# Running both gate/up products of a pair of expert items ahead of its transposes and down products

## The chip, the cores and the metric

The kernel runs on one core of one Trainium2 chip. The metric is the device time of one execution in microseconds (us), given as the median of the runs shown. The durations below come from one profiled execution of the same kernel.

## What is computed

One inference step of a two-layer decoder on 256 prompt tokens and 8 x 4 sample tokens, T = 288 tokens of width D = 1024 in all. Layer 0 mixes tokens with a chunked spatial-gating MLP, layer 1 with block-sparse attention over a paged cache. Each mixer is followed by a mixture of experts, which is the part this change touches:

```python
# x: the 288 normalised tokens; 16 experts, two per token, all inside one group of four
a   = einsum('nd,edf->nef', x, w_gate)      # w_gate, w_up: 16 x 1024 x 256
b   = einsum('nd,edf->nef', x, w_up)
hid = silu(a) * b * gates[:, :, None]       # gates: zero but for the two chosen experts
y   = einsum('nef,efd->nd', hid, w_down)    # w_down: 16 x 256 x 1024
h   = h + y
```

Everything is float32. One expert's weights are 1 MB (gate), 1 MB (up) and 1 MB (down).

## The kernel before

**Items and pairs.** The tokens of an expert are served in *items* of up to 64 slots. Each of the 16 experts has one item; experts with more than 64 tokens get further items, planned at run time. Items are worked in pairs `i`, with `u` = 0 and 1 and the running number `q = 2i + u`. In the profiled execution layer 0 has 16 items (8 pairs) and layer 1 has 18 (9 pairs); each L1090 group of 32 matmuls is one item. A float32 matmul of the source counts as two instructions.

**One item on TensorE** (`pair`, L1080 to L1109). It waits for the item's gate and up weights, for the transposed token rows `x_slotsT[:, u]` (`xt_sb`) and for the `hid` tile of two items before. Then come the gate/up products (L1090, 32 instructions into bank 2+u). After the first item of a pair stands `table_of(i + 3)` (L1061, 12 small matmuls that make the index table of a later pair). Then `rows_up` (L1070) transposes the gathered token rows of the *next* item. Then two transposes of `hid` (L1101, into bank 4) and, after DVE has copied them to `hidT`, the down products (L1108, 8 instructions into bank 5+u). `dn` is raised at their end. TensorE works in program order.

**One item on ACT** (`experts`, L576 to L583). It waits for `gu`, makes `silu` (L580), waits for `dn` of the *same* item, then for the scatter that last used the buffer, and copies the result to `y_slots` (L583). Then comes the next item. `ready_for(ACT.Silu)` (L549) loads the table once in a pair.

**One item on DVE** (L846 to L854). `hid` = `silu` x up x gate (L848) once `silued` is raised, `x_tile` (L828: the next item's transposed rows out of PSUM), the copy to `hidT` (L852), and the copy of the output indices (L854). At the end of a pair stands the index arithmetic of pair `i+3` (L798 to L807), at its beginning a one-hot of 6 instructions (L780).

**One pair on POOL** (L477 to L494). For u = 0 and 1: wait until the earlier gather has landed, copy the indices (L462), wait until `rows_up` has emptied the buffer (`xt`), and issue the gather of the *next pair's* rows (L466, 128 half rows of 2 KB, an indirect DMA). Then for u = 0 and 1: wait for the copy of L583 and issue the scatter (L492). The loop then starts again, so the next pair's gathers stand behind this pair's second scatter.

**Weights.** SP issues the loads. There are four sets of weight buffers: `ew_in`/`ew_down` (two) and the halves `pre_in`/`pre_down` (two). The first four items' weights are loaded before the expert stage. Items 4 and 5 go to `ew`, 6 and 7 to the halves, and all from item 8 on to the two `ew` buffers alone. A gate/up load is issued when the products that last read its buffer are done (`hold(gu)`), a down load likewise (`hold(dn)`). The order is in(u=0), down(0), in(1), down(1). So the loads of items 4 to 7 are released by items 0 to 3, those of 8 and 9 by items 4 and 5, and those of 10 by item 8.

**Before and behind.** Ahead of the loop TensorE makes two tables and the transposes of item 0's rows (`rows_up(0, 16, 0)`). After the last pair SP waits for the last scatters and loads the rows of `y` back.

## Time and profile before

| | |
|---|---|
| median of 3 runs | 822.12 us (822.06 to 829.37) |
| span of the profiled execution | 826.3 us |
| TensorE (PE) busy | 642.1 us, 78% |
| DVE busy | 291.2 us, 35% |
| ACT busy | 160.0 us, 19% |
| POOL busy | 138.6 us, 17% |
| moved by DMA | 187.77 MB, mean 227 GB/s |
| on the chain that ended last | PE 61%, DMA 15%, DVE 10% |

The span of the profiled execution lies between the fastest and the slowest of the runs, 4.2 us above their median. Busy shares are means over stages with different limits, so the table says little of the expert stages by itself; they run from about 185 to 317 us (layer 0) and from 648 to 798 us (layer 1). Matmul ends are modelled, and a matmul group can overlap the one before it by some 0.1 us.

### The profile page before, as it was taken

The page shows a single profiled execution, that of the slowest core. Times are in us where ns is not written, and L with a number is a line of the kernel's source. Part 1 is how long each engine was busy: PE and PEld are TensorE (multiplying, and loading weights), DVE is VectorE, ACT ScalarE, POOL GpSimd, SP SyncE. Part 2 cuts the span into 40 slices and gives each one's busy share as a digit, 9 for nine tenths or more (in the row PEclk, how much of TensorE's full clock was granted, in tenths as well). Part 3 has the DMA queues.
Part 4 walks back from the last instruction along what each step waited for, and adds up shares of the span by engine and source line. Part 5 has one row for each costly group of instructions (what it writes and reads, how often), then busy time and mean ns, then how long its engine had stood idle before and what let it go on. Part 6 is the DMA issues. An engine that isn't in the chain of part 4 may idle for free.

```text
span 826.3 us, 12476 instructions
## 1 busy us (share of the span) xinstructions
PE 642.1 (78%) x4123; PEld 435.9 (53%) x4123; DVE 291.2 (35%) x916; ACT 160.0 (19%) x336; POOL 138.6 (17%) x224
## 2 busy tenths in 40 slices
PE   5899999839888763799988857766987788876740
PEld 3677667525555442576667526445765455534420
DVE  2202211473334221537747341332126443333214
ACT  2123101111212111111125321211113121222100
POOL 0000000022323220131114001420000223222212
PEclk9999959968999997599999986976998799999995
DMA  9964400426999994970019563973923399999933
GB/s 349 288 229 175 137 23 1 153 72 235 369 369 314 371 360 147 402 304 0 1 52 367 179 212 128 337 268 152 349 81 132 118 370 374 324 374 366 361 127 123
DMA packets 114729, 187.77 MB, mean 227 GB/s; under 512 B 11996, under 2 KB 82190, under 8 KB 114694
## 3 DMA queue, kind: packets, MB, share of 16 engines
q1 hardware_dynamic: 103174, 158.71, 55.4%
q0 software_dynamic: 11520, 28.60, 9.5%
q8 instruction: 20, 0.33, 0.2%
q14 instruction: 15, 0.12, 0.0%
HBM read 182.95 MB, written 13.76 MB: 238 GB/s over the span
## 4 chain that ended last, share of the span: by engine, by line
PE 61%; DMA 15%; DVE 10%; issue 5%; SPq 5%; ACT 3%; DVEq 0%; POOLq 0%; ACTq 0%
PE PS L1005 24%; PE PS L1090 12%; DMA ew_in<-in_moe_w_up 10%; PE PS L1108 5%; PE PS L996 3%; PE PS L1301 2%; DMA half_a<-in_cache_k 2%; DMA zT<-y_rows 2%; SPq L292 2%; SPq L305 2%; PE PS L1176 1%; PE PS L1265 1%; PE PS L1021 1%; SPq L294 1%; PE PS L1061 1%
## 5 line engine op out<-in xcount | busy, mean ns | idle before, releaser
L1090 PE MATMUL PS<-ew_in,zT 128*64 128x256 f32 x832 | 99.8, 394 | 21.9 <-DMA ew_in<-in_moe_w_up 18.7
L1005 PE MATMUL PS<-hT,half_a 128*128 128x288 f32 x384 | 98.1, 414 | 4.0 <-DVE hT L678 3.1
L1090 PEld LDWEIGHTS PS<-ew_in,zT 128*64 128x64 f32 x832 | 67.4, 142 | 62.4 <-issue 43.7
L1005 PEld LDWEIGHTS PS<-hT,half_a 128*128 128x128 f32 x384 | 73.2, 193 | 27.8 <-issue 3.7
L848 DVE SCALAR_TENSOR_TENSOR zT<-PS,slot_gates,zT 64x256 f32<-64x256 f32 x34 | 16.5, 485 | 163.6 <-ACT zT L580 159.1
L1005 PE MATMUL PS<-hT,half_b 128*128 128x288 f32 x256 | 66.9, 421 | 3.3 <-DVE hT L678 3.3
L1108 PE MATMUL PS<-ew_down,zT 128*64 128x512 f32 x208 | 50.4, 601 | 17.3 <-issue 17.3
L492 POOL DMA_INDIRECT y_rows<-zT,out_idx x34 | 34.3, 1010 | 155.7 <-ACT zT L583 155.7
L1005 PEld LDWEIGHTS PS<-hT,half_b 128*128 128x128 f32 x256 | 50.1, 197 | 19.5 <-issue 3.7
L1265 PE MATMUL PS<-cst,half_a 128*128 128x128 f32 x256 | 40.3, 308 | 17.7 <-DMA half_a<-in_cache_k 10.2
L1265 PEld LDWEIGHTS PS<-cst,half_a 128*128 128x128 f32 x256 | 32.1, 157 | 33.3 <-issue 15.5
L466 POOL DMA_INDIRECT zT<-h_rows,in_idx x38 | 39.7, 1045 | 58.5 <-PE PS L1070 27.0
L583 ACT COPY zT<-PS 128x512 f32<-128x512 f32 x34 | 19.9, 585 | 125.5 <-PE PS L1108 125.5
L472 POOL DMA_DIRECT2D h_rows<-tokbuf x2 | 1.7, 830 | 244.7 <-ACT tokbuf L571 244.7
L549 ACT ACT_TABLE_LOAD x24 | 30.8, 1283 | 25.6 <-DVE pairs L820 24.4
L555 ACT ACTIVATE sq<-xT 128x288 f32<-128x288 f32 x32 | 13.6, 442 | 112.9 <-DVE xT L685 86.0
L1005 PE MATMUL PS<-zT,half_a 128*128 128x288 f32 x128 | 34.1, 426 | 0.0
L1108 PEld LDWEIGHTS PS<-ew_down,zT 128*64 128x64 f32 x208 | 14.9, 136 | 33.5 <-issue 33.5
L580 ACT ACTIVATE zT<-PS 64x256 f32<-64x256 f32 x34 | 12.8, 377 | 100.2 <-PE PS L1090 100.2
L675 DVE RECIPROCAL rec<-std 128x288 f32<-128x288 f32 x5 | 9.8, 1953 | 57.6 <-ACT std L559 57.6
L1005 PEld LDWEIGHTS PS<-zT,half_a 128*128 128x128 f32 x128 | 25.6, 201 | 7.4
L685 DVE TENSOR_TENSOR xT<-PS,xT 128x288 f32<-128x288 f32 x16 | 7.3, 457 | 61.8 <-PE PS L1005 61.8
(234 smaller groups left out, 892.5 us busy)
## 6 DMA issues: line engine op xcount, KB each, us to landing
ew_in<-in_moe_w_gate SPq DMA_DIRECT2D x26, 1024.0 KB
ew_in<-in_moe_w_up SPq DMA_DIRECT2D x26, 1024.0 KB
ew_down<-in_moe_w_down SPq DMA_DIRECT2D x26, 1024.0 KB, 12.4
half_a<-in_cache_k SPq DMA_DIRECT2D x64, 256.0 KB, 4.0
ew_in<-in_cache_v POOLq DMA_DIRECT2D x32, 256.0 KB, 6.8
half_b<-in_cache_v POOLq DMA_DIRECT2D x32, 256.0 KB, 5.6
half_a<-in_a_w_in SPq DMA_DIRECT2D x1, 4096.0 KB, 15.2
half_b<-in_a_w_in SPq DMA_DIRECT2D x1, 4096.0 KB, 25.3
```

The lines of the kernel that those rows point to most:

```text
L292: at = [eng.value_load(pages[0:1, bass.ds(b * NPAGE + j, 1)], min_val=0, max_val=NPOOL - 1) for j in pp]
L305: sp.dma_start(dst, src).then_inc(s, 16)
L466: pool.indirect_dma_start(out=x_slots[:, u, :], out_offset=None, in_=h_dram.rearrange("t (h n) -> (t h) n", h=2), in_offset=bass.IndirectO ...
L492: pool.indirect_dma_start(out=y_dram[l].rearrange("t k (h n) -> (t k h) n", h=2), out_offset=bass.IndirectOffsetOnAxis(ap=out_idx[u][:, 0: ...
L549: act.activation(spare[:, :], eps[:, :], func)
L583: act.copy(y_slots[:, u, :], PS[:, 5 + u, :]).then_inc(E[l]["y_sb"], 1)
L996: mm = pe.matmul(PS[:, 7, 0:T], mean_d[:, :], sq[:, k, :], start=(k == 0), stop=(k == KT - 1))
L1005: mm = pe.matmul(PS[:, bank, 0:T], w[:, k, col:col + P], src[:, k, :], start=(k == 0), stop=(k == KT - 1))
L1090: mm = pe.matmul(PS[f * SLOT:(f + 1) * SLOT, 2 + u, 0:EF], x_slotsT[:, u, k % 4, k // 4, :], w_in[u][:, k, f, :], start=(k == 0), stop=(k ...
L1108: mm = pe.matmul(PS[half * SLOT:(half + 1) * SLOT, 5 + u, :], hidT[:, f, :], w_down[u][:, f, half * HALF:(half + 1) * HALF], start=(f == 0 ...
L1265: mm = pe.transpose(PS[:, n % 2, a * P:(a + 1) * P], k_pages[:, bb % 2, n % NPAGE, a * P:(a + 1) * P], ident)
L1301: mm = pe.matmul(PS[a * HR:(a + 1) * HR, 5, bb * P:(bb + 1) * P], PdT[:, j, a * HR:(a + 1) * HR], v_pages[bb][:, j, a * P:(a + 1) * P], st ...
```

## The change

In each pair TensorE now does: gate/up of item 0, gate/up of item 1, the table, then for each item the `hid` transposes, `rows_up`, and the down products. `rows_up` now serves the item two further on, `q + 2`, with the same `u`, and waits for that item's gather, `in{u}` at `16 * (i + 2)`; so `rows_up(1, 16, 1)` and `x_tile(1, 2)` are added ahead of the loop. On DVE `x_tile` comes behind the copy to `hidT` instead of ahead of it. ACT gets one more wait, since both `silu` share a buffer; its order is otherwise as it was. POOL's code is unchanged. SP's loads come in the order in(0), in(1), down(0), down(1). The last wait before the `y` rows are loaded counts one tile more.

```diff
--- before.py
+++ after.py
@@ -349,33 +349,33 @@
 
 
                 with sp.Fori(1, QUADS) as i:
-                    for u in range(4):
-
-                        w_in, w_down = (ew_in, ew_down) if u < 2 else (pre_in, pre_down)
-                        hold(E[l]["gu"], 4 * i - 3 + u)
-                        expert_in(l, 4 * i + u, w_in[u % 2], E[l][f"w{u}"] if u < 2 else s_pre[u % 2])
-                        hold(E[l]["dn"], 4 * i - 3 + u)
-                        expert_down(l, 4 * i + u, w_down[u % 2], E[l][f"wd{u}"] if u < 2 else s_pre[u % 2])
-
-                def item(e, u, before):
-
-                    hold(E[l]["gu"], before + 1)
-                    expert_in(l, e, ew_in[u], E[l][f"w{u}"])
-                    hold(E[l]["dn"], before + 1)
-                    expert_down(l, e, ew_down[u], E[l][f"wd{u}"])
-
-                for u in range(2):
-                    item(4 * QUADS + u, u, 4 * QUADS - 4 + u)
+                    for half in range(2):
+                        w_in, w_down = (pre_in, pre_down) if half else (ew_in, ew_down)
+                        for u in range(2):
+                            hold(E[l]["gu"], 4 * i - 3 + 2 * half + u)
+                            expert_in(l, 4 * i + 2 * half + u, w_in[u], s_pre[u] if half else E[l][f"w{u}"])
+                        for u in range(2):
+                            hold(E[l]["dn"], 4 * i - 3 + 2 * half + u)
+                            expert_down(l, 4 * i + 2 * half + u, w_down[u], s_pre[u] if half else E[l][f"wd{u}"])
+
+                def two(experts, before):
+
+                    for u in range(2):
+                        hold(E[l]["gu"], before + u + 1)
+                        expert_in(l, experts[u], ew_in[u], E[l][f"w{u}"])
+                    for u in range(2):
+                        hold(E[l]["dn"], before + u + 1)
+                        expert_down(l, experts[u], ew_down[u], E[l][f"wd{u}"])
+
+                two([4 * QUADS, 4 * QUADS + 1], 4 * QUADS - 4)
                 sp.wait_ge(E[l]["planned"], 1)
                 n = sp.value_load(pairs[0:1, 0:1], min_val=NE // 2, max_val=NE // 2 + 5)
                 with sp.Fori(2 * QUADS + 1, n) as i:
-                    for u in range(2):
-                        e = sp.value_load(items[0:1, bass.ds(2 * i + u, 1)], min_val=0, max_val=NE - 1)
-                        item(e, u, 2 * i - 2 + u)
+                    two([sp.value_load(items[0:1, bass.ds(2 * i + u, 1)], min_val=0, max_val=NE - 1) for u in range(2)], 2 * i - 2)
                 for u in range(2):
                     hold(E[l][f"sc{u}"], 16 * n + 16)
                     hold(E[l][f"in{u}"], 16 * n + 16)
-                hold(E[l]["xt_sb"], AHEAD["xt_sb"] + 2 * n + 1)
+                hold(E[l]["xt_sb"], AHEAD["xt_sb"] + 2 * n + 2)
                 for c, (at, m) in enumerate(tok):
                     for k, dst in enumerate((tokbuf, y_second)):
                         load(dst[0:m, c, :], y_dram[l][at:at + m, k, :], s_yb[c])
@@ -577,6 +577,7 @@
                     ready_for(ACT.Silu)
                     for u in range(2):
                         act.wait_ge(E[l]["gu"], 2 * i + u + 1)
+                        act.wait_ge(E[l]["hid"], AHEAD["hid"] + 2 * i + u)
                         act.activation(silu, PS[0:SLOT, 2 + u, 0:EF], ACT.Silu).then_inc(E[l]["silued"], 1)
                         act.wait_ge(E[l]["dn"], 2 * i + u + 1)
                         act.wait_ge(E[l][f"sc{u}"], 16 * i + 16)
@@ -836,6 +837,7 @@
                 plan(l)
                 n = dve.value_load(pairs[0:1, 0:1], min_val=NE // 2, max_val=NE // 2 + 5)
                 x_tile(0, 1)
+                x_tile(1, 2)
                 with dve.Fori(0, n) as i:
                     shift(l, 1, 2 * i + 2)
                     shift(l, 2, 2 * i + 3)
@@ -847,9 +849,9 @@
                         dve.wait_ge(el["silued"], q + 1)
                         dve.scalar_tensor_tensor(out=hid, in0=PS[SLOT:2 * SLOT, 2 + u, 0:EF], scalar=slot_gates[0:SLOT, 0, u:u + 1],
                                                  in1=silu, op0=ALU.mult, op1=ALU.mult).then_inc(el["hid"], 1)
-                        x_tile(1 - u, q + 2)
                         dve.wait_ge(el["ht"], q + 1)
                         dve.tensor_copy(hidT, PS[:, 4, 0:FB * SLOT].rearrange("p (f n) -> p f n", f=FB)).then_inc(el["ht_sb"], 1)
+                        x_tile(u, q + 3)
                         dve.wait_ge(el[f"sc{u}"], 16 * i + 16)
                         dve.tensor_copy(out_idx[u][:, :], outs[:, 0, u:u + 1]).then_inc(el["out"], 1)
                     indices(l, i + 3, ISTEPS * (i + 2))
@@ -1074,54 +1076,64 @@
                 pe.wait_ge(el["idx"], 1)
                 table_of(2)
                 rows_up(0, 16, 0)
+                rows_up(1, 16, 1)
                 pe.wait_ge(el["planned"], 1)
                 pairs_n = pe.value_load(pairs[0:1, 0:1], min_val=NE // 2, max_val=NE // 2 + 5)
 
+                def gate_up(i, u, w_in, weights):
+
+                    q = 2 * i + u
+                    weights(u, False)
+                    pe.wait_ge(el["xt_sb"], AHEAD["xt_sb"] + q + 1)
+                    pe.wait_ge(el["hid"], q + 1)
+                    for k in range(KT):
+                        for f in range(2):
+                            mm = pe.matmul(PS[f * SLOT:(f + 1) * SLOT, 2 + u, 0:EF], x_slotsT[:, u, k % 4, k // 4, :],
+                                           w_in[u][:, k, f, :], start=(k == 0), stop=(k == KT - 1))
+                    mm.then_inc(el["gu"], 1)
+
+                def down(i, u, w_down, weights):
+
+                    q = 2 * i + u
+                    pe.wait_ge(el["hid"], AHEAD["hid"] + q + 1)
+                    pe.wait_ge(el["ht_sb"], AHEAD["ht_sb"] + q)
+                    pe.sem_inc(S["held"], 1)
+                    for f in range(FB):
+                        mm = pe.transpose(PS[:, 4, f * SLOT:(f + 1) * SLOT], hid[:, f * P:(f + 1) * P], ident[0:SLOT, 0:SLOT])
+                    mm.then_inc(el["ht"], 1)
+                    rows_up(u, 16 * (i + 2), q + 2)
+                    weights(u, True)
+                    pe.wait_ge(el["ht_sb"], AHEAD["ht_sb"] + q + 1)
+                    pe.wait_ge(el["y_sb"], q + 1)
+                    for f in range(FB):
+                        for half in range(2):
+                            mm = pe.matmul(PS[half * SLOT:(half + 1) * SLOT, 5 + u, :], hidT[:, f, :],
+                                           w_down[u][:, f, half * HALF:(half + 1) * HALF], start=(f == 0), stop=(f == FB - 1))
+                    mm.then_inc(el["dn"], 1)
+
+                def streamed(u, down, loads):
+
+                    pe.wait_ge(el[f"wd{u}"] if down else el[f"w{u}"], 16 * loads if down else 32 * loads)
+
+                def in_halves(u, down, loads):
+
+                    if not down:
+                        pe.wait_ge(s_pre[u], 48 * loads)
+
                 def pair(i, w_in, w_down, weights):
 
                     for u in range(2):
-                        q = 2 * i + u
-
-                        weights(u, False)
-                        pe.wait_ge(el["xt_sb"], AHEAD["xt_sb"] + q + 1)
-                        pe.wait_ge(el["hid"], q + 1)
-                        for k in range(KT):
-                            for f in range(2):
-                                mm = pe.matmul(PS[f * SLOT:(f + 1) * SLOT, 2 + u, 0:EF], x_slotsT[:, u, k % 4, k // 4, :],
-                                               w_in[u][:, k, f, :], start=(k == 0), stop=(k == KT - 1))
-                        mm.then_inc(el["gu"], 1)
-                        if u == 0:
-                            pe.wait_ge(el["idx"], i + 2)
-                            table_of(i + 3)
-                        rows_up(1 - u, 16 * (i + 1 + u), q + 1)
-                        pe.wait_ge(el["hid"], AHEAD["hid"] + q + 1)
-                        pe.wait_ge(el["ht_sb"], AHEAD["ht_sb"] + q)
-                        pe.sem_inc(S["held"], 1)
-                        for f in range(FB):
-                            mm = pe.transpose(PS[:, 4, f * SLOT:(f + 1) * SLOT], hid[:, f * P:(f + 1) * P], ident[0:SLOT, 0:SLOT])
-                        mm.then_inc(el["ht"], 1)
-                        weights(u, True)
-                        pe.wait_ge(el["ht_sb"], AHEAD["ht_sb"] + q + 1)
-                        pe.wait_ge(el["y_sb"], q + 1)
-                        for f in range(FB):
-                            for half in range(2):
-                                mm = pe.matmul(PS[half * SLOT:(half + 1) * SLOT, 5 + u, :], hidT[:, f, :],
-                                               w_down[u][:, f, half * HALF:(half + 1) * HALF], start=(f == 0), stop=(f == FB - 1))
-                        mm.then_inc(el["dn"], 1)
-
-                def streamed(loads):
-
-                    return ew_in, ew_down, lambda u, down: pe.wait_ge(el[f"wd{u}"] if down else el[f"w{u}"], 16 * loads if down else 32 * loads)
-
-                def in_halves(loads):
-                    return pre_in, pre_down, lambda u, down: None if down else pe.wait_ge(s_pre[u], 48 * loads)
-
+                        gate_up(i, u, w_in, weights)
+                    pe.wait_ge(el["idx"], i + 2)
+                    table_of(i + 3)
+                    for u in range(2):
+                        down(i, u, w_down, weights)
 
                 with pe.Fori(0, QUADS) as i:
-                    pair(2 * i, *streamed(i + 1))
-                    pair(2 * i + 1, *in_halves(l * QUADS + i + 1))
+                    pair(2 * i, ew_in, ew_down, lambda u, down: streamed(u, down, i + 1))
+                    pair(2 * i + 1, pre_in, pre_down, lambda u, down: in_halves(u, down, l * QUADS + i + 1))
                 with pe.Fori(2 * QUADS, pairs_n) as i:
-                    pair(i, *streamed(i + 1 - QUADS))
+                    pair(i, ew_in, ew_down, lambda u, down: streamed(u, down, i + 1 - QUADS))
 
             pe.wait_ge(S["const_in"], 16)
             pe.wait_ge(S["x_in"], 32)
```

## Rows read from the trace of the kernel before

**Rows 1.** Windows of layer 0: busy by engine, granted clock, DMA share, GB/s

```profile
203.40:248.20 44.80, 39.50 (x315) 23.56 (x312) 16.96 (x78) 10.23 (x18) 13.48 (x18) 1.00 1.08 369
248.20:254.00 5.80, 5.04 (x54) 3.29 (x50) 2.96 (x13) 2.45 (x4) 2.44 (x4) 1.00 0.52 182
254.00:311.60 57.60, 44.57 (x342) 26.59 (x344) 16.77 (x75) 10.81 (x19) 15.52 (x20) 1.00 1.04 359
```

**Rows 2.** The same windows view, layer 1

```profile
664.90:709.70 44.80, 39.49 (x314) 23.52 (x312) 16.82 (x75) 10.23 (x18) 13.52 (x18) 1.00 1.07 372
709.70:715.40 5.70, 4.94 (x52) 3.23 (x48) 2.86 (x11) 2.45 (x4) 2.44 (x4) 1.00 0.60 222
772.60:790.00 17.40, 13.58 (x104) 7.83 (x105) 5.59 (x25) 3.41 (x6) 4.50 (x6) 1.00 1.01 344
```

**Rows 3.** Chain that ended last, layer 0: start, us, what

```profile
203.41 3.45 PE PS L1090 x32
...
248.21 3.45 PE PS L1090 x32
...
309.25 3.69 PE PS L1090 x32
314.88 1.95 PE PS L1108 x8
```

**Rows 4.** The same chain, layer 1

```profile
664.88 3.45 PE PS L1090 x32
...
709.68 3.45 PE PS L1090 x32
```

**Rows 5.** Timeline of one pair: start, us, engine, line, operation, [idle before <-releaser]

```profile
206.79 0.70 PE L1061 MATMUL PS<-marks,zT 128*128 128x6 bf16 x12
206.90 0.38 ACT L580 ACTIVATE zT<-PS 64x256 f32<-64x256 f32 x1 [1.35 <-PE PS L1090]
...
207.43 0.66 PE L1070 MATMUL PS<-cst,zT 128*128 128x128 f32 x4
...
209.07 1.94 PE L1108 MATMUL PS<-half_a,zT 128*64 128x512 f32 x8 [0.71 <-DVE zT L852]
...
211.13 0.58 ACT L583 COPY zT<-PS 128x512 f32<-128x512 f32 x1 [3.85 <-PE PS L1108]
...
214.92 0.48 DVE L848 SCALAR_TENSOR_TENSOR zT<-PS,slot_gates,zT 64x256 f32<-64x256 f32 x1 [5.84 <-ACT zT L580]
...
215.55 0.30 PE L1101 MATMUL PS<-cst,zT 64*128 64x64 f32 x2 [0.50 <-DVE zT L848]
216.04 0.28 DVE L852 COPY zT<-PS 128x128 f32<-128x128 f32 x1
...
216.38 1.94 PE L1108 MATMUL PS<-half_b,zT 128*64 128x512 f32 x8 [0.52 <-DVE zT L852]
```

**Rows 6.** Timeline of POOL at the seam of two pairs

```profile
204.91 1.00 POOL L492 DMA_INDIRECT y_rows<-zT,out_idx  x1 [6.21 <-ACT zT L583]
205.91 0.20 POOL L462 COPY in_idx<-row_idx 128x1 int32<-128x1 int32 x1
207.16 1.05 POOL L466 DMA_INDIRECT zT<-h_rows,in_idx  x1 [1.06 <-issue]
```

**Rows 7.** Gathers of L466, issue to landing, from 176 to 184 us

```profile
DMA to landing us min/median/max: 2.8/2.8/2.8
```

**Rows 8.** Gathers of L466, issue to landing, from 203 to 245 us

```profile
DMA to landing us min/median/max: 6.0/6.1/6.4
```

**Rows 9.** The one gather of L466 issued at 193.96 us, issue to landing

```profile
DMA to landing us min/median/max: 7.7/7.7/7.7
```

**Rows 10.** Timeline of the start of layer 0's expert stage

```profile
181.90 1.04 POOL L466 DMA_INDIRECT zT<-h_rows,in_idx  x1 [0.87 <-POOL in_idx L462]
...
182.93 1.12 PE L1070 MATMUL PS<-cst,zT 128*128 128x128 f32 x4 [1.68 <-DMA zT<-h_rows,in_idx]
...
185.54 6.34 PE L1090 MATMUL PS<-ew_in,zT 128*64 128x256 f32 x32 [1.50 <-DVE zT L828]
```

## The prediction, made before the changed kernel was run

> **What bounds the kernel now.** I read the windows view first, because a busy share over the whole span hides the stages. Each expert stage falls into parts. From the first pair on the DMA engines are full while TensorE works through prefetched weights: the three pairs from 203.4 to 248.2 us move 369 GB/s at a DMA share of 1.08 [rows 1], and layer 1 does the same [rows 2]. Then there is a hole at the seam: 5.8 us at a share of 0.52 in layer 0 and 5.7 us at 0.60 in layer 1 [rows 1, 2]. Against the full share of 1.08 that is 5.8 x (1 - 0.52/1.08) = 3.0 us and 5.7 x (1 - 0.60/1.07) = 2.5 us of idle DMA. The hole is there because item 10's weights may only be loaded when item 8's gate/up products are done, and the timeline of TensorE sets when that is. After it, DMA is full again for 57.6 us (359 GB/s) and TensorE waits [rows 1].
>
> So two things set the length of an expert stage: **X, the time at which item 8's gate/up products end** (all the loads behind it then take the same time as before), and the **tail** from the last gate/up weights to the last down product. What TensorE does between the seam and the tail is covered, if a pair of it takes less than DMA's pair. DMA's pair is at its shortest 17.4 us [rows 2].
>
> The chain view gives X: pairs 1, 2 and 3 take 248.21 - 203.41 = 44.80 us, 14.93 us each [rows 3], and 44.80 us again in layer 1 [rows 4].
>
> **The pair after, step by step.** Let e be the end of the down products of the pair before.
>
> *What goes away.* In the pair of now TensorE idles 0.71 us ahead of the first down product, 0.50 us ahead of the second item's transposes and 0.52 us ahead of its down products [rows 5]: 1.73 us. After the change item 0's silu and `hid` are made under item 1's gate/up products (3.45 us [rows 3] against 0.38 + 0.48 us and their hand-overs [rows 5]), and the copy to `hidT` (0.28 us) lies under `rows_up` (0.66 us), for both items. So all three waits go, and a fourth must be looked for.
>
> *What comes.* ACT's order is unchanged: silu of item 0, wait for item 0's down products, copy y, and only then silu of item 1. So although item 1's gate/up products are long done, its chain starts only behind item 0's down products, and TensorE has nothing queued ahead of item 1's transposes that could cover it. From the rows of one pair: down products to the copy of y 211.13 - 211.01 = 0.12 us, the copy 0.58 us, silu 0.38 us, the hand-over to DVE some 0.04 us, `hid` 0.48 us, the hand-over to the transposes 215.55 - 215.40 = 0.15 us [rows 5]. With the step from copy to silu on ACT that is about 1.77 us. It takes the place of the 1.73 us removed, so the reordering by itself gives nothing.
>
> *Natural length without any DMA wait.* Gate/up 3.45 + 3.47, table 0.64, transposes 0.29, `rows_up` 0.60 (the last two net of overlap), down 1.94, chain 1.77, transposes 0.31, `rows_up` 0.60, down 1.94: 15.01 us, against 14.93 now. Bounds of the exposed chain: 1.7 us from the rows, 0 if ACT's copy could be passed, which its order excludes.
>
> *The moved `rows_up`, and POOL's queue.* This is the term that decides. The gathers of the next pair's rows are issued on POOL behind the second scatter of the pair before, and that order is unchanged. Now: scatter at 204.91 us, 1.00 us long, index copy, gather at 207.16 us [rows 6], that is e + 3.75 us with e = 203.41 [rows 3]. With DMA full such a gather lands 6.0 to 6.4 us after issue, 6.1 us at the median [rows 8], so at e + 9.85 us. Today its first reader is the `rows_up` behind the *second* item's gate/up products, shortly before that item's `hid` at 214.92 us [rows 5] and so near e + 11 us; the wait is hidden. After the change the first reader is `rows_up(0)`, which stands ahead of item 0's down products: it is due at 3.45 + 3.47 + 0.64 + 0.29 = e + 7.85 us. TensorE waits 9.9 - 7.85 = **2.05 to 2.2 us**, with the down products, y, silu and `hid` of item 1 and the next scatter all behind it. The second scatter then is later as well, and so is the next gather: the wait comes back in each pair. I take 2.1 us and the 0.08 us of the natural length, 2.2 us a pair, a period of 17.1 us. The other gather, issued 2.3 us later, is read after the down products and the chain, and is hidden.
>
> The bounds of this wait: with DMA idle gathers land in 2.8 us [rows 7], ready at e + 6.6, no wait; one, issued just as the first load began, took 7.7 us [rows 9], a wait of 3.7 us. The row nearest to the changed kernel's pairs 1 to 3 is rows 8, with the same loads in flight, so I take 6.1 us.
>
> [...]
>
> *Which pairs count.* Pair 0 does not: its gathers for pair 1 are issued at the start of the loop, where DMA is idle, and the gate/up products of item 0 run 6.34 us at the lower clock [rows 10]. Pairs 1, 2 and 3 count fully, since X lies right behind them: 3 x 2.2 = 6.6 us. From pair 4 on the wait costs nothing as long as 17.1 us is below DMA's pair; at the shortest 17.4 us that still holds, though closely.
>
> *Start.* `rows_up(1)` now stands ahead of the loop. Its gather is issued at 181.90 us and lands about 2.8 us later, at 184.7; the transposes take 1.12 us as the first ones do [rows 7, 10], to 185.8, against the start of gate/up at 185.54 [rows 10]: 0.3 us. `x_tile(1)` is on DVE, not in the way.
>
> *Tail.* From the start of the last gate/up products to the end of the last down products it is now 314.88 + 1.95 - 309.25 = 7.58 us [rows 3]. After: 3.69 + 0.64 + 0.29 + 0.60 + 1.94 + 1.77 + 0.31 + 0.60 + 1.94 = 11.8 us, 4.2 us more. Against it, in(1) no longer stands behind down(0) in SP's queue: it lands earlier by one down load, 1.05 MB at 359 GB/s = 2.9 us. Net 1.3 us. Bounds: 0.5 us (if the hand-overs overlap more) to 4.2 us (if the earlier landing is lost).
>
> *SP's new order elsewhere.* The second in-load is issued some 4 us sooner, the first down load some 3 us later. With DMA full this only reorders a full queue, and down(0) is still released 7 us or more before DMA comes to it. I cost it at nothing; the cover is the queue of loads, and without it each of these would be a hole of up to 3 us. DVE's index work starts some 1 us later in a pair, but its result is wanted only behind the second gate/up products.
>
> **Sum.** Per layer 0.3 + 6.6 + 1.3 = 8.2 us, for both 16.4 us. The profiled span goes from 826.3 to 842.7 us. That execution lies 4.2 us above the median of the runs; with the same difference added to the median, 822.1 + 16.4 = **838.5 us**.
>
> **The rivals.**
>
> *Not slower: the gathers land in time.* The wait at `rows_up(0)` falls away if a gather under the new load order lands in under about 4.1 us. Then a layer pays 0.3 + 3 x 0.08 + 1.3 = 1.8 us, and the kernel takes 822.1 + 3.7 = 825.8 us. For it: an idle DMA gives 2.8 us [rows 7]. Against it: DMA is as full in these pairs as it was [rows 1, 2], and all six gathers of that window took at least 6.0 us [rows 8]. It decides from a latency of 4.8 us downwards: there the wait is 0.8 us, and 2 x (0.3 + 3 x 0.8 + 1.3) = 8 us is about 1%. Chance 0.13.
>
> *Much slower: gathers take longer, or DMA runs dry behind X.* With 7.7 us [rows 9] the wait is 3.7 us: 2 x (0.3 + 3 x 3.8 + 1.3) = 26 us, 848 us; the period of 18.7 us would then also exceed DMA's shortest pair of 17.4 us [rows 2] and open more holes. Against it: that row is the one gather that met the very first load. Chance 0.12.
>
> *Faster: the pair gets shorter.* If item 1's chain were covered after all, a pair would be 1.8 us shorter and X would come some 5 us sooner. But DMA then has no hole left, and only the holes can be gained: 3.0 + 2.5 = 5.5 us in all, less the tails: 822.1 - 5.5 + 2 x 1.3 = 819.2 us. A gain over 1% is thus closed off by the loads. Chance 0.05, nearly all within 1%.
>
> **How the numbers follow.** The case of the 2.2 us has a chance of 0.70. Its own range is 833 to 844 us (a wait of 1.5 to 2.8 us a pair, tails of 0.5 to 2 us). The range that should hold 8 times in 10 takes in the first rival's end nearly and the second one's centre: 826 to 848 us. About 1%, 8 us, is what a measurement of this kernel can tell from no change. Slower by over 1%: 0.70 + 0.12 = 0.82, less a little for a short wait, 0.81; within 1% 0.17; faster 0.02.
>
> **What the changed profile should show.** (1) The period of pairs 1 to 3 is 17.1 us instead of 14.93; the natural one would be 15.0. (2) TensorE idles about 2.1 us ahead of L1070 in each of these pairs, with the gather as releaser, and gathers still land about 6.1 us after issue at e + 3.75. (3) About 1.8 us idle ahead of the second item's transposes, with silu of L580 right behind the copy of L583 on ACT. (4) None of the old waits ahead of the down products. (5) The hole in DMA at the seam grows from 3.0 and 2.5 us to about 9 us in each layer, and the DMA-full part behind it is as long as before. (6) The tail is near 11.8 us. The prediction is wrong if gathers are issued earlier in the pair than e + 3.75 or land much sooner, or if DMA in the changed order falls short of 359 GB/s behind the seam.

## The result and the profile after

The changed kernel takes **856.94 us** (854.04 to 861.43, 4 runs) against 822.09 us before: a ratio of 1.045, 95% interval 1.040 to 1.050. It is slower, as forecast, but by 34.8 us instead of 16.4, and outside the range. Its profiled execution spans 859.7 us, 33.4 us more than the one before. From the first gate/up products to the last down products layer 0 takes 330.1 - 186.0 = 144.1 us (131.3 before) and layer 1 takes 831.4 - 662.3 = 169.1 us (149.9 before), 12.8 and 19.2 us more; so nearly all of it is in the two expert stages. The stretch between them, whose code no version here changes, takes 332 us (331 before) and between 321 and 333 us in the profiles below, so profiles are best compared by stages. Each time is the median of all runs shown; each ratio is against runs of the kernel before made at the same time, and leaves out runs over 1.5% above the fastest of their kernel.

The first pair under full loads, from the timeline (start, us, engine, line, operation, idle before and its releaser). L1102 are the `hid` transposes, L1072 is `rows_up`, L1110 the down products, L581 silu, L584 the copy of y:

```profile
207.13 1.05 POOL L466 DMA_INDIRECT zT<-h_rows,in_idx  x1 [1.06 <-issue]
...
213.16 0.65 PE L1072 MATMUL PS<-cst,zT 128*128 128x128 f32 x4 [1.98 <-DMA zT<-h_rows,in_idx]
213.74 1.94 PE L1110 MATMUL PS<-half_a,zT 128*64 128x512 f32 x8
...
215.80 0.58 ACT L584 COPY zT<-PS 128x512 f32<-128x512 f32 x1 [8.48 <-PE PS L1110]
216.28 0.38 ACT L581 ACTIVATE zT<-PS 64x256 f32<-64x256 f32 x1
...
217.33 0.31 PE L1102 MATMUL PS<-cst,zT 64*128 64x64 f32 x2 [1.65 <-DVE zT L850]
...
218.15 3.55 PE L1110 MATMUL PS<-half_b,zT 128*64 128x512 f32 x8
```

The two waits of the prediction are at their places: 1.98 us ahead of `rows_up`, released by the gather that POOL issued at 207.13 us, and 1.65 us ahead of item 1's transposes, with silu right behind the copy of y on ACT. (The wait for the gather is 2.40 and 0.87 us in pairs 2 and 3.) The last line is what the prediction did not have: the same 8 instructions that took 1.94 us [rows 5] take 3.55 us, at a granted clock of 0.53 from 218.15 to 221.70 us. The windows view of the changed kernel shows why (columns as in [rows 1]; the number behind POOL's is the granted clock, then DMA share and GB/s): pairs 1 to 3 of layer 0 and pair 4, then the same pairs of layer 1.

```profile
203.40:257.90 54.50, 44.30 (x315) 23.41 (x313) 17.43 (x76) 9.92 (x19) 13.48 (x18) 0.91 0.91 319
257.90:278.90 21.00, 16.67 (x106) 8.30 (x104) 7.10 (x33) 3.34 (x7) 4.49 (x6) 0.78 0.83 272
...
679.00:737.40 58.40, 47.38 (x316) 23.98 (x313) 18.80 (x83) 9.92 (x18) 13.59 (x18) 0.85 0.87 302
737.40:759.60 22.20, 17.57 (x106) 8.63 (x104) 5.79 (x27) 3.31 (x6) 4.50 (x6) 0.73 0.81 269
```

Before, the granted clock was 1.00 in every window of [rows 1, 2]. Now it falls for stretches inside the stages: it is 1.00 from 204 to 218 us, 0.50 from 232 to 234 us and 0.50 again from 270 to 278 us. Pairs 1 to 3 take 54.5 / 3 = 18.2 us in layer 0 and 58.4 / 3 = 19.5 us in layer 1, and pair 4 takes 21.0 and 22.2 us. In layer 0 the sum of pairs 1 to 3 closes: three natural lengths of 15.0 us, waits for the gather of 1.98 + 2.40 + 0.87 = 5.3 us, and down products of 3.55, 3.09 and 3.52 us in place of 1.94, which is 4.3 us more; together 54.6 us, against 54.5 measured.

The hole in DMA at the seam, in windows that hold all of it:

```profile
250.00:263.00 13.00, 10.48 (x77) 5.73 (x78) 5.94 (x25) 3.31 (x6) 3.46 (x5) 1.00 0.12 33
726.00:747.40 21.40, 16.19 (x104) 8.20 (x104) 5.78 (x25) 3.31 (x6) 4.50 (x6) 0.84 0.31 105
```

Against the full share that is 13.0 x (1 - 0.12/1.08) = 11.6 us and 21.4 x (1 - 0.31/1.07) = 15.2 us of idle DMA, where it was 3.0 and 2.5 us. The low share of pair 4 is mostly the end of this hole. Behind it DMA is full at first, and then, as pair 4 ends late, it falls short a second time:

```profile
262.60:276.00 13.40, 9.06 (x54) 4.19 (x52) 2.58 (x8) 0.86 (x2) 2.31 (x4) 0.76 1.06 334
276.00:288.00 12.00, 11.57 (x90) 6.51 (x86) 3.49 (x19) 2.45 (x4) 3.47 (x5) 0.84 0.86 294
```

That is 12.0 x (1 - 0.86/1.08) = 2.4 us more of idle DMA in layer 0; in layer 1 the share is 0.72 from 756 to 768 us.

### The profile page after: what moved, and what is told of

Same layout as the page of the kernel before. It is cut to its first block, busy times and chain, and to the rows that moved or that the text cites. A ratio compares the mean times of both kernels' runs of the same rounds, so it can differ in the third digit from the quotient of the medians.

```text
span 859.7 us, 12517 instructions
## 1 busy us (share of the span) xinstructions
PE 668.8 (78%) x4131; PEld 435.2 (51%) x4131; DVE 296.4 (34%) x918; ACT 158.3 (18%) x336; POOL 138.8 (16%) x224
## 4 chain that ended last, share of the span: by engine, by line
PE 57%; DMA 18%; DVE 8%; issue 8%; SPq 4%; ACT 4%; POOL 1%; POOLq 1%; ACTq 0%; DVEq 0%
PE PS L1007 23%; PE PS L1110 9%; DMA zT<-h_rows,in_idx 8%; PE PS L1091 5%; DMA ew_in<-in_moe_w_up 4%; PE PS L998 3%; PE PS L1072 3%; PE PS L1313 2%; DMA zT<-y_rows 2%; DMA half_a<-in_cache_k 2%; SPq L292 2%; PE PS L1188 1%; SPq L294 1%; PE PS L1277 1%; SPq L305 1%
## 5 line engine op out<-in xcount | busy, mean ns | idle before, releaser
L1091 PE MATMUL PS<-ew_in,zT 128*64 128x256 f32 x832 | 103.3, 409 | 9.1 <-DMA ew_in<-in_moe_w_up 7.8
L1091 PEld LDWEIGHTS PS<-ew_in,zT 128*64 128x64 f32 x832 | 64.9, 150 | 55.6 <-issue 29.1
L1007 PEld LDWEIGHTS PS<-hT,half_a 128*128 128x128 f32 x384 | 73.2, 193 | 27.8 <-issue 3.7
L1110 PE MATMUL PS<-ew_down,zT 128*64 128x512 f32 x208 | 63.7, 743 | 0.0
L584 ACT COPY zT<-PS 128x512 f32<-128x512 f32 x34 | 19.9, 585 | 224.3 <-PE PS L1110 224.3
L1277 PE MATMUL PS<-cst,half_a 128*128 128x128 f32 x256 | 38.1, 296 | 18.1 <-DMA half_a<-in_cache_k 9.6
L1072 PE MATMUL PS<-cst,zT 128*128 128x128 f32 x152 | 29.2, 323 | 24.2 <-DMA zT<-h_rows,in_idx 24.1
L1277 PEld LDWEIGHTS PS<-cst,half_a 128*128 128x128 f32 x256 | 29.9, 149 | 33.3 <-issue 15.2
L466 POOL DMA_INDIRECT zT<-h_rows,in_idx x38 | 39.7, 1044 | 39.8 <-issue 33.1
L829 DVE COPY zT<-PS 128x512 f32<-128x512 f32 x38 | 26.3, 691 | 35.2 <-PE PS L1072 33.9
L853 DVE COPY zT<-PS 128x128 f32<-128x128 f32 x34 | 9.9, 292 | 78.8 <-PE PS L1102 78.8
L1102 PE MATMUL PS<-cst,zT 64*128 64x64 f32 x68 | 11.2, 245 | 28.9 <-DVE zT L850 28.9
L1072 PEld LDWEIGHTS PS<-cst,zT 128*128 128x128 f32 x152 | 18.6, 158 | 28.3 <-DMA zT<-h_rows,in_idx 26.6
## 6 DMA issues: line engine op xcount, KB each, us to landing
half_a<-in_a_w_in SPq DMA_DIRECT2D x1, 4096.0 KB, 15.2
```

The lines of the kernel that those rows point to most:

```text
L466: pool.indirect_dma_start(out=x_slots[:, u, :], out_offset=None, in_=h_dram.rearrange("t (h n) -> (t h) n", h=2), in_offset=bass.IndirectO ...
L584: act.copy(y_slots[:, u, :], PS[:, 5 + u, :]).then_inc(E[l]["y_sb"], 1)
L829: dve.tensor_copy(x_slotsT[:, u], PS[:, u, :].rearrange("p (j h n) -> p j h n", j=4, h=2)).then_inc(el["xt_sb"], 1)
L1007: mm = pe.matmul(PS[:, bank, 0:T], w[:, k, col:col + P], src[:, k, :], start=(k == 0), stop=(k == KT - 1))
L1072: mm = pe.transpose(PS[:, u, j * P:(j + 1) * P], x_slots[:, u, j * P:(j + 1) * P], ident)
L1091: mm = pe.matmul(PS[f * SLOT:(f + 1) * SLOT, 2 + u, 0:EF], x_slotsT[:, u, k % 4, k // 4, :], w_in[u][:, k, f, :], start=(k == 0), stop=(k ...
```

## The experiments

My theory after the result: the two waits are real and as large as forecast, and they also let TensorE's clock fall, which makes up the part that the sum missed ("clock"). The rivals: the clock is a bystander and the waits cost more than I counted ("waits alone"), or SP's new order of loads is the loss ("load order"). Lines in the fences are those of each kernel's own code; the operands tell which operation it is.

### Filling the idle places with matmuls nobody reads

```diff
+                def filler(n):
+                    for _ in range(n):
+                        pe.matmul(PS[:, 7, 256:512], ident, cst[:, 0:256], start=True, stop=True)
...
                     mm.then_inc(el["ht"], 1)
+                    if u == 0:
+                        filler(8)
                     rows_up(u, 16 * (i + 2), q + 2)
...
                     mm.then_inc(el["dn"], 1)
+                    if u == 0:
+                        filler(7)
```

> The changed kernel with filler matmuls on TensorE in its two idle places of each pair: 8 float32 matmuls of 128x256 (about 1.75 us at full clock) behind item 0's transposes, ahead of the wait for the gather, and 7 (about 1.5 us) behind item 0's down products, ahead of item 1's transposes. They write an unused part of PSUM and nothing reads them, so all waits stay where they are. Theory 'clock': the two waits of about 2 us a pair let the granted clock fall in the expert stages (0.78 to 0.91 in windows of the changed kernel, 1.00 before), and the slow matmuls make up what my sum missed. Then the fillers bring the clock of these windows back to about 1.00, the down products to 1.94 us each, a pair to about 17 us, and the time from 857 to 838-845 us. Rival 'waits alone': the missing part is DMA running dry in the new load order, and the clock is a bystander. Then the fillers change the time by less than 4 us, or add a little.

Measured: 886.2 us. I had sized the filler wrongly: one filler instruction takes 0.23 us, where 1.75 us for 16 is 0.11 us, the pace of the gate/up products (3.45 us for 32 [rows 3]). The timeline of TensorE and the windows view:

```profile
216.11 3.72 PE L1098 MATMUL PS<-cst 128*128 128x256 f32 x16
```

```profile
200.00:258.00 58.00, 58.00 (x398) 37.97 (x397) 17.84 (x75) 9.92 (x18) 13.48 (x18) 1.00 0.96 318
```

The filler pushed the work behind it, so the time says nothing on the theories. One thing can be read all the same: TensorE is never idle and the clock is at 1.00, in pairs that are *longer* (19.7 us) than the changed kernel's. Half the filler was the right size, `filler(4)` and `filler(3)`:

> As a_fill, with half the filler: 4 and 3 float32 matmuls of 128x256. In a_fill one filler instruction took 0.235 us (16 took 3.72 us, 14 took 3.29 us), twice what I had counted, so that kernel's pairs were 19.7 us by the fillers alone, though the clock was at its upper level from 190 to 351 us. Here 8 x 0.235 = 1.9 us and 6 x 0.235 = 1.4 us just fit in the two idle places. Theory 'clock': clock 1.00 in the expert stages, a pair of 17.0 to 17.4 us, time 838-845 us against 857. Rival 'waits alone': 853 us or more.

Measured: **843.5 us** (ratio 1.027, 1.023 to 1.030), 13.4 us less than the changed kernel, by adding work. Windows of pairs 1 to 3 of layer 0, and what is left of the wait for the gather in the second of them, from the timeline:

```profile
204.30:254.90 50.60, 49.41 (x356) 29.52 (x354) 17.77 (x76) 9.92 (x18) 13.48 (x18) 1.00 0.95 331
```

```profile
231.05 0.66 PE L1072 MATMUL PS<-cst,zT 128*128 128x128 f32 x4 [0.45 <-DMA zT<-h_rows,in_idx]
```

The gather is still the releaser, so the wait is still there, behind the filler; the clock is 1.00, where it was 0.91 without the filler, and a pair takes 50.6 / 3 = 16.9 us, near the 17.1 us of the sum. That settles "clock" against "waits alone" in this kernel. The filler is not free where no wait stands for it to fill: in the last pair of layer 0 gate/up of item 1 to the last down product takes 326.5 - 313.2 = 13.2 us here and 11.6 us in the changed kernel.

### Taking the wait for the gather away

POOL's loop is turned by half, so that the next pair's first gather goes out ahead of the last pair's second scatter (`fetch` and `scatter` hold the code of the old loop body):

```diff
-                with pool.Fori(0, n) as i:
-                    ...  # both fetches of pair i, then both scatters of pair i
+                hold(E[l]["idx"], 2)
+                fetch(0, 0)
+                fetch(0, 1)
+                scatter(0, 0)
+                with pool.Fori(1, n) as i:
+                    hold(E[l]["idx"], i + 2)
+                    fetch(i, 0)
+                    scatter(i - 1, 1)
+                    fetch(i, 1)
+                    scatter(i, 0)
+                scatter(n - 1, 1)
```

> The changed kernel with POOL's loop turned by half: the next pair's gather for u=0 is issued ahead of the last pair's second scatter, at about e + 1.2 us (e: the end of a pair's down products) in place of e + 3.75. The gather still takes about 6.1 us under full DMA. Theory 'gather wait': it lands at e + 7.3 to 7.5, before rows_up(0) is due at e + 7.85, so the 2 us wait ahead of L1072 goes, and a pair takes about 15.0 us with one idle place of 1.65 us left (silu of item 1 behind the copy of y). If the clock falls only with both waits it is back at 1.00, and the time is 824-830 us. If a single idle place of 1.65 us a pair is enough to lower it, a pair takes 15.5 to 16.5 us and the time is 832-842 us. Rival 'load order': the loss is in SP's order, then the time stays above 845 us though the wait is gone.

Measured: 832.9 us (ratio 1.013, 1.009 to 1.016), 24 us less than the changed kernel, in the range named for "a single idle place is enough to lower the clock"; a pair takes 15.8 us in layer 0, also as named for it. POOL at the seam, and TensorE behind it:

```profile
204.76 1.05 POOL L466 DMA_INDIRECT zT<-h_rows,in_idx  x1 [1.07 <-issue]
206.12 1.01 POOL L491 DMA_INDIRECT y_rows<-zT,out_idx  x1 [0.31 <-issue]
```

```profile
211.31 0.66 PE L1083 MATMUL PS<-cst,zT 128*128 128x128 f32 x4 [0.29 <-DMA zT<-h_rows,in_idx]
...
215.48 0.31 PE L1113 MATMUL PS<-cst,zT 64*128 64x64 f32 x2 [1.65 <-DVE zT L861]
```

The gather is issued 2.4 us earlier (204.76 against 207.13) and the wait shrinks from 1.98 to 0.29 us. The 1.65 us of item 1's chain are left, and the window of 203 to 248 us has a clock of 0.96. With the small filler of three matmuls in that one place:

> a_gather (the wait for the gather gone, 832.9 us, low-clock stretches in both expert stages) with the small filler of 3 matmuls (6 instructions, 1.4 us) in its one idle place, behind item 0's down products. The filler writes an unused part of PSUM. Theory 'clock': one idle place of 1.65 us a pair is enough to lower the clock, and this is what kept a_gather above the natural 825.8 us of my sum; then the clock is full in the stages and the time 822-829 us. If the clock was not the reason: 832 us or more. Against a_fill2 (843.5 us, both waits there, full clock) this one then gives the price of the gather wait alone at full clock: my sum had 2 x 3 x 2.1 = 12.6 us.

Measured: **823.5 us** (ratio 1.004, 0.999 to 1.008), 9.4 us less than without the filler; window 203 to 248 us:

```profile
203.00:248.00 45.00, 44.26 (x338) 25.49 (x336) 18.27 (x79) 10.03 (x19) 13.70 (x19) 1.00 1.07 371
```

So the reordered TensorE program with the gather in time and the clock kept up is within measurement of the kernel before: the reordering by itself gives nothing, as the prediction had it (825.8 us in the first rival). Against `a_fill2` this prices the gather wait at full clock. In pairs 1 to 3 of layer 0 a pair is 14.8 us here (down products ending at 203.49 and 247.85 us, three pairs apart) and 16.9 us there: 2.1 us a pair, the number of the sum. The whole kernel shows more than the 12.6 us of the sum: the medians differ by 20.0 us, the expert stages of the two profiles by 6.6 and 8.5 us, of which the filler in the last pair has some 1.6 us in layer 0. The remaining 5 us lie outside the stages and stay unexplained.

### Hiding item 1's chain instead

```diff
                         act.activation(silu, PS[0:SLOT, 2 + u, 0:EF], ACT.Silu).then_inc(E[l]["silued"], 1)
+                    for u in range(2):
                         act.wait_ge(E[l]["dn"], 2 * i + u + 1)
```

> The changed kernel with ACT's order changed: both silu first, then both copies of y. Item 1's chain (copy, silu, hid: 1.65 us idle ahead of L1102) then lies under the table and item 0's down products. The gather is still issued at e + 3.75 and lands at about e + 9.9, so rows_up(0) waits 2.0 us as before. A pair is 9.9 + 0.60 + 1.94 + 0.31 + 0.60 + 1.94 = 15.3 us. Theory 'clock': with one idle place of 2 us left the clock is mostly full and the time is 826-834 us. If one place is enough to lower it: 835-845 us. Rival 'load order': above 845 us.

Measured: 834.4 us (ratio 1.016, 1.010 to 1.022). The wait for the gather stands alone, and is as large as before:

```profile
229.37 0.66 PE L1073 MATMUL PS<-cst,zT 128*128 128x128 f32 x4 [2.18 <-DMA zT<-h_rows,in_idx]
```

The clock is 0.89 from 203 to 248 us. The time lies at the edge between the two cases that I had named, so the clock was pinned with the filler:

> a_act (item 1's chain hidden, the gather wait of 2.1 us there, 834.4 us) with the filler of 4 matmuls (8 instructions, 1.9 us) in the gather wait. Theory 'clock': full clock in the stages, a pair of 15.3 us, 821-827 us. If the clock was not the reason: 833 us or more.

Measured: 831.1 us (ratio 1.015, 1.009 to 1.021), 4 us above my range. The ratio is that of `a_act`, so no gain in time is shown. The clock of 203 to 248 us is 1.00 again, and pairs 1 to 3 of layer 0 are shorter: 15.2 us each (down products ending at 203.0 and 248.7 us) against 16.7 us (201.5 and 251.5). But this is lost behind them: both expert stages together take 284.9 us in the profile, against 284.5 without the filler. In layer 1 the stretch from the last gate/up products to the last down products is 13.2 us with it and 9.8 us without. Of these 3.4 us some 1.9 are the filler, whose place has no wait to fill there, as in `a_fill2`, and most of the rest are the last gate/up products, 5.36 us at a clock of 0.68 in place of 3.67 at 1.00; how much of the whole loss the filler is was not separated.

### Putting `rows_up(0)` where TensorE is idle anyway

```diff
-                    rows_up(u, 16 * (i + 2), q + 2)
+                    if u == 1:
+                        rows_up(u, 16 * (i + 2), q + 2)
...
                     mm.then_inc(el["dn"], 1)
+                    if u == 0:
+                        rows_up(u, 16 * (i + 2), q + 2)
```

> The changed kernel with one move on TensorE alone: rows_up(0), which waits for the gather, stands behind item 0's down products, where TensorE is idle anyway while ACT and DVE make item 1's hid. POOL, ACT, DVE and SP as changed. If the wait for the gather is what costs, and only because the down products and all of item 1's chain stand behind it, both waits now lie over each other: down products from e + 8.3 (after the copy to hidT) to e + 10.2, the gather lands at e + 9.9, hid of item 1 at about e + 12.1, item 1's transposes at e + 12.3, a pair of 15.1 to 15.3 us. Time 824-834 us. If the wait costs by delaying POOL's next gather alone, whatever it covers, the time stays near 857.

Measured: 836.7 us (ratio 1.016, 1.008 to 1.023), 20 us less than the changed kernel by one move on TensorE, though 3 us above my range (a pair takes 15.6 us in layer 0, against 15.1 to 15.3); its clock is 0.96 from 203 to 248 us. POOL still issues the gather behind the second scatter, and in pairs 1 to 3 `rows_up(0)` waits for it once, for 0.29 us, so what costs is what is queued *behind* the wait, and not the wait for the gather as such.

### Undoing the order of the loads alone

```diff
                             expert_in(l, 4 * i + 2 * half + u, w_in[u], s_pre[u] if half else E[l][f"w{u}"])
-                        for u in range(2):
                             hold(E[l]["dn"], 4 * i - 3 + 2 * half + u)
```

(and the same in `two`)

> The changed kernel with SP's order of loads as before the change: in(0), down(0), in(1), down(1). All of TensorE, ACT, DVE and POOL as changed. Theory 'gather wait and clock': the order of loads in a full queue matters little, and in(1) now stands behind down(0), which costs a few us in the tails and at the seam: 855-866 us. Rival 'load order': if the new order is what let DMA run dry (share 0.83 and 0.95 in the pairs behind the seam), undoing it gives 6 us or more back: below 851 us.

Measured: 881.7 us (ratio 1.075, 1.068 to 1.082), **25 us more** than the changed kernel. Neither number that I had written holds: the old order is not the cure, and it is not nearly neutral either. In the kernel with both remedies (below) it costs more still:

> a_both (earlier gather, both silu first) with SP's old order of loads. In a_both TensorE waits for in-loads and DMA bounds the stage. The second gate/up stands right behind the first now, so in(1) is wanted sooner than down(0). Theory 'order fits the work': the old order costs 1 to 3 us a layer in the tail (in(1) lands one down load of 2.9 us later): 818-824 us against 816.9. Rival 'order is nothing': within 2 us of 816.9.

Measured: 855.5 us against 816.9, again far above my range. The trace of this second kernel, `both_order`, shows the chain best, as it has hardly any other wait. Who SP waits for in layer 0 (in us, times, longest), in the kernel before and in `both_order`; L1108 and L1120 are the down products:

```profile
SPq L310 <- PE PS L1108: 11.7, 6, 3.1
```

```profile
SPq L310 <- PE PS L1120: 38.7, 6, 11.6
```

And the chain in the timelines of SP and TensorE of `both_order`:

```profile
248.24 0.53 SPq L305 DMA_DIRECT2D ew_in<-in_moe_w_up  x1
258.51 0.37 SPq L305 DMA_DIRECT2D ew_down<-in_moe_w_down  x1
259.13 0.37 SPq L305 DMA_DIRECT2D ew_in<-in_moe_w_gate  x1
```

```profile
272.04 6.48 PE L1101 MATMUL PS<-ew_in,zT 128*64 128x256 f32 x32 [7.53 <-DMA ew_in<-in_moe_w_up]
```

In the old order down(0) stands ahead of in(1) on SP, and SP waits for item 0's down products, which now come only behind item 1's gate/up. So item 1's next weights, whose buffer is long free, are issued at 259.13 us instead of right behind their products, which end at 255.0 us, and TensorE waits 7.53 us for them (at most 3.8 us in the same kernel with the new order). In `a_order` the same wait is 4.5 to 5.1 us in six of the pairs. The order of loads is no freight of the change: it is what makes the order of the products possible.

### Both remedies

The earlier gather on POOL and both silu ahead of both copies on ACT, all else as in the changed kernel:

> The changed kernel with both edits: the gather issued earlier on POOL and both silu ahead of both copies on ACT. No wait of TensorE should be left in a pair: 3.45 + 3.47 + 0.64 + 0.29 + 0.60 + 1.94 + 0.31 + 0.60 + 1.94 = 13.2 to 13.5 us, with a small wait for the gather possible (due at e + 7.85, landing at e + 7.3 to 7.6). X comes about 4.5 us sooner than before the change, so the holes in DMA at the seam (3.0 and 2.5 us) close and DMA bounds the expert stages from their first load on; the tail is near 10.0 - 2.9 = 7.1 us against 7.6. Expected 815-819 us, below the kernel before (822.1). If DMA in the new order is less efficient, or pairs are held by weights, no better than 822 us.

Measured: **816.85 us** (10 runs; ratio to the kernel before 0.991, 0.987 to 0.994), 40 us less than the changed kernel. The medians lie 5.4 us below the kernel before, and the ratio says 7.6 us (4.6 to 10.5). The profiled execution took 822.8 us, 5.9 us above the median. TensorE's waits in layer 0 (us in total, times, longest), and two windows:

```profile
PE PS L1103 <- DMA ew_in<-in_moe_w_up: 13.4, 6, 3.8
...
PE PS L1084 <- DMA zT<-h_rows,in_idx: 2.1, 4, 0.8
```

```profile
203.00:248.00 45.00, 42.47 (x344) 24.19 (x342) 19.50 (x84) 11.43 (x20) 15.81 (x21) 1.00 1.07 372
250.00:300.00 50.00, 38.82 (x274) 20.40 (x270) 16.72 (x72) 9.86 (x17) 11.18 (x15) 0.93 1.07 366
```

The hole at the seam is gone (share 1.07 on both sides, and 1.05 from 248 to 254 us). A pair of layer 0 takes 14.0 us, not the 13.2 to 13.5 expected, as small waits for the gather and for weights are left. Behind the seam DMA is full, so the fall of TensorE's clock there (0.93) should cost little; that was not tested. The gain is of the size of the 5.5 us of idle DMA that the prediction named as all that can be gained.

The expert stages of all profiled executions, each from the first gate/up products to the last down products, in us:

| kernel | layer 0 | layer 1 | sum, less that of before |
|---|---|---|---|
| before | 131.3 | 149.9 | |
| changed | 144.1 | 169.1 | +32.0 |
| `a_fill` | 159.5 | 180.5 | +58.8 |
| `a_fill2` | 140.2 | 159.8 | +18.8 |
| `a_gather` | 135.3 | 153.4 | +7.5 |
| `gather_fill` | 133.6 | 151.3 | +3.7 |
| `a_act` | 134.6 | 149.9 | +3.3 |
| `act_fill` | 131.9 | 153.0 | +3.7 |
| `a_behind` | 133.4 | 156.2 | +8.4 |
| `a_order` | 153.5 | 176.6 | +48.9 |
| `both_order` | 142.7 | 166.3 | +27.8 |
| `a_both` | 129.5 | 148.5 | -3.2 |

The prediction's sum was +16.4 for the changed kernel, +3.7 with the gathers in time and -2.9 for the case of a shorter pair.

## Why the prediction was right or wrong, point by point

- **The reordering alone gives nothing:** right. The old waits ahead of the down products are gone and 1.65 us ahead of item 1's transposes came in their place (1.77 forecast). `gather_fill` is within measurement of the kernel before.
- **The gather at e + 3.75, the wait of 2.05 to 2.2 us:** right. It is issued at 207.13 us with e = 203.4, and the wait is 1.98 us in the first pair and 2.40 us in the second. In the third, whose gather is under way as DMA runs dry (share 0.65 from 248 to 250 us, 0.17 from 250 to 252), it is only 0.87 us. Removing the wait with the filler at work is worth 2.1 us a pair.
- **The period of 17.1 us:** right at full clock (16.9 in `a_fill2`), wrong in the changed kernel (18.2 in layer 0, and in layer 1, where pairs 0 to 3 end at 679.0 and 737.4 us, 19.5). **This is the step that failed.** Every duration of a pair in the sum was taken from rows at a clock of 1.00 and carried over to a kernel with two idle places of about 2 us a pair. The before kernel idles 1.73 us a pair as well, but in three pieces of 0.5 to 0.7 us; that the pieces would become two long ones was in my own sum, and I asked only what they cost in time, not what they do to the clock, which stands in the sum at nothing. What the runs showed in its place: products at the lower clock, 4.3 us of them in pairs 1 to 3 of layer 0, and 13.4 us in the whole kernel, which came back when the filler kept the clock up (856.9 to 843.5 us).
- **Behind the seam the wait costs nothing, as 17.1 is below 17.4 us:** wrong for the same reason. I had called it close. At 21.0 us pair 4 is above DMA's pair, DMA falls short once more (294 GB/s from 276 to 288 us, the prediction's own sign of being wrong), and the loss goes on behind X: X is 9.6 us later in layer 0 (261.3 against 251.7), the end of the stage 13.3 us. Behind X that is 3.7 us, the 1.3 us of the sum and the 2.4 us of this second gap. In the changed kernel TensorE never waits for weights in layer 0 behind X; with the clock kept up it does again in the last two pairs (0.87 and 2.88 us in `a_fill2`).
- **The hole of about 9 us in each layer:** too small: 11.6 and 15.2 us.
- **The tail of 11.8 us:** right in layer 0: the last gate/up products start at 318.5 us and the last down products end at 330.1, 11.6 us. In layer 1 it is 13.2 us, as the last gate/up products take 5.36 us there, at a clock of 0.68.
- **SP's new order at nothing:** right as a price as far as `gather_fill` shows it (+3.7 us in the stages, as in the sum), wrong in its reason. I named a queue of loads as cover and "a hole of up to 3 us" as what it would cost without it. Undone, it costs 25 us, and not by DMA's queue but by SP's: a load waits behind another load's condition (259.13 us in `both_order`, for products that ended at 255.0).
- **The rivals:** the gather in time did not happen by itself, but made to happen it gave 823.5 us at full clock, against 825.8. "Much slower" (848 us) came nearest, and its pairs longer than DMA's and its further holes came true, but from the clock and not from gathers of 7.7 us; none of the three named the clock. The bound on any gain, 5.5 us, is not contradicted: the best version gains 5.4 us by medians and 4.6 to 10.5 us by the ratio, too wide to confirm it.

A sum of 838.5 us was thus a fair forecast of the kernel with the clock held up, which took 843.5 us with the filler in it. Of the 5.0 us between them 1.6 us is the filler in the last pair of layer 0; the rest was not separated. The 13.4 us above 843.5 are the clock, as far as the filler prices it.

## What to carry to other kernels

When the order of one engine's work is changed, walk the other in-order queues with it. Here ACT (copy of y ahead of the second silu, 1.65 us of idle TensorE in a pair), POOL (scatter ahead of the next gather, 1.98 and 2.40 us in two of the pairs) and SP (one load's condition ahead of another load, 7.53 us in one pair of `both_order`) each had an order that fitted the old one; SP's was changed too, and the other two turned a neutral reordering into a loss of 4.5%, and with both fixed it is a gain of 0.9% (0.6 to 1.3%).

A sum made of durations from rows at full clock holds only if the clock stays full: the same 8 instructions took 1.94 us at 1.00 and 3.55 us at 0.53. The busy share alone does not tell: TensorE was busy 77% of the time at a clock of 1.00 from 254.0 to 311.6 us before [rows 1], and 81% at 0.91 in pairs 1 to 3 of the changed kernel. If the change gathers small idle pieces into one of 2 us a pair, work out a second sum with part of the products at the lower clock, and put its result in the range. How much of the lost clock reached the kernel's time differed: 13.4 us in the changed kernel, 9.4 in `a_gather`, none that can be measured in `a_act`. That what bounds the stage decides this is my reading, and no run shows it.

## What the hardware showed that I had not expected

- Idle places of 1.65 us in a pair of 15.8 us were enough here to lower the granted clock at times (`a_gather`: 0.96 over 45 us; with 1.4 us of filler in the same place 1.00 and 9.4 us less time). With two such places it is 0.91 in pairs 1 to 3 of layer 0 and 0.85 in those of layer 1. Three pieces of 0.5 to 0.7 us left it at 1.00 [rows 1, 5]. Which spacing is tolerated stays open: in the DMA-bound part of the kernel before, TensorE waited too (busy 44.57 of 57.6 us [rows 1]), and the clock stayed at 1.00.
- Matmuls whose result nobody reads made a kernel 1.6% faster (856.9 to 843.5 us), and twice as many made it 3.4% slower (886.2).
- A gather under full loads lands about 6 us after issue, also when it is issued earlier in the pair: 6.2 us at the median in `a_gather` and in `a_both`, and 6.1 us before [rows 8]. In the changed kernel the median is 5.9 us from 203 to 262 us, with 3.0 us at the least, as the window holds the hole at the seam.
